# A matmul of 272 and one of 256 columns in place of two of 264, with x in rows of high and low

## Chip, cores and metric

One core of one Trainium2 chip. The metric is device time in microseconds (us) of one launch; the time before is 2108.19 us, the median of 3 runs (2107.79 to 2108.54).

## The reference

One step of a one-layer decoder for 264 tokens (256 of a prompt and 8 single ones), width 2048, all in fp32. A mixer (input projection to 7168, short gated convolution and retention, output projection) is followed by PEER, a retrieval of experts, and a last RMSNorm. What matters here is PEER's sum over experts:

```
u = u_tab[idx]
act = gelu(einsum('td,thkd->thk', xb, u))
w = gate * act
out = einsum('thk,thkd->td', w, v_tab[idx])
```

The table has 16384 experts, each with a row u and a row v of 2048. The kernel doesn't gather: it computes `x U^T` for all experts, takes the gelu, multiplies by a gate that is zero where a token didn't pick the expert, and multiplies the result by V.

## The kernel before

All activations lie transposed: 128 features or experts on the partitions, the 264 tokens (`T`) as columns. Every large product is made in three matmuls of type fp32r. An operand is split into a high part (the value rounded to fp32r) and a low part (the rest), and `half` adds `high x high`, `low weight x high` and `high weight x low` in PSUM. A weight tile is 128 output features by 2048 inputs, loaded in two halves of 8 rows of 128 x 128 (512 KB each, 688 halves in all). The path of a half: SP's queue loads it into `raw`, a ring of 4 (L523, L539); ScalarE casts it to `whi` (L640); VectorE subtracts and writes `wlo` (L1192); TensorE goes through the 8 rows with three matmuls each (L940, L941, L942). `lo_done` releases TensorE and the next load, `half_used` releases ScalarE's next cast. `whi` and `wlo` have a pitch of 136 words a row (`PITCH`), and all x operands are read from the last column to the first.

Stages, in order: heads' projections with retention beside them (moving operand `xghi`, `xglo`), the convolution's, the output projection (`xhi`, `xlo`), the queries (`xghi`, `xglo`), then PEER. In PEER a u tile (2 halves, 16 rows) gives 128 experts' scores in one bank; 7 groups of 8 u tiles lead, and 9 rounds (`MIXED`) follow, of 8 u tiles and 8 v tiles each; the last 7 groups have v tiles alone. A v group has 8 tiles of 2 halves with 8 rows, one row for each of the group's 8 expert tiles; each half fills one bank with one chunk j of the output, and VectorE adds the bank into `acc[:, j]` (`add_out`, L1827). So v's stages have 16 groups x 8 x 2 x 8 = 2048 rows. Their moving operand is the gated hidden value, in `wexp_hi` and `wexp_lo` in the mixed rounds and, in the last 7 groups, in halves of `xhi` and `xlo` (`expanded`; written at L884 and L1821 by ScalarE and VectorE in `weigh_hi` and `weigh`).

TensorE's other work is small: sums over partitions with plain fp32 (L972, L1020, L1024), turns and attention (L984 to L1013), query scores (L1068), and batches of 24 bf16 matmuls of 64 columns that build the gates (L1113).

Order on the engines is written out by hand: in each tile step, `ahead(r, k)` comes first and converts the two halves after next, then come gelu, gates and adds of the tile before. Banks 0 to 3 take turns for outputs; `bank_free` releases them.

x arrives in `acc` by four loads (`x_block`, L520); at the end `acc` is scaled and stored in six (L1883, L561).

Of the kernel before, what the change touches and what calls it, by code (L numbers as in the profile page):

```python
# [20 lines left out]
F32 = mybir.dt.float32  # L21
# [24 lines left out]

PITCH = P + T % P

SQ_RING = 4
# [161 lines left out]
def build(nc, halves, xT, conv_state, ret_state, norm_mix, conv_w, gn_g, gn_b, norm_ffn, keysT, norm_fin,  # L211
          consts, out_yT, out_conv, out_pret, out_sret):
    with ExitStack() as ctx:
        def sb(name, shape, dt=F32, scope=ctx):
            return scope.enter_context(nc.sbuf_tensor(name, shape, dt))
# [8 lines left out]

        xhi = sb("xhi", [P, CH, T], F32R)
        xlo = sb("xlo", [P, CH, T], F32R)
        acc = sb("acc", [P, CH, T])
        keep = sb("keep", [P, KEEP])
# [19 lines left out]

        xghi = sb("xghi", [P, CH, T], F32R, mix)
        xglo = sb("xglo", [P, CH, T], F32R, mix)  # L250
        tables = sb("tables", [P, NCONST - KEEP], F32, mix)
# [46 lines left out]
        scope.close()  # L298
        wexp_hi = sb("wexp_hi", [P, GROUP, T], F32R)
        wexp_lo = sb("wexp_lo", [P, GROUP, T], F32R)  # L300

# [197 lines left out]
        def wait_gates(eng, half):  # L499
            for i in range(2):  # L500
                eng.wait_ge(gates_stored[i], 16 * stored_of((half + 1) * BLOCKS, i))

        def expanded(buf):

            if buf is None:
                return wexp_hi, wexp_lo
            return xhi[:, buf * GROUP:(buf + 1) * GROUP], xlo[:, buf * GROUP:(buf + 1) * GROUP]

# [418 lines left out]
        def _(pe):  # L927
            def from_last(x):
                return x[..., ::-1] if len(x.shape) == 2 else x.rearrange("p a t -> p (a t)")[:, ::-1]

            def half(r, off, out, mh, ml, start, stop, waits=()):

                s = off % RING
                pe.wait_ge(lo_done, RING * r + off + 1)
                back = out[:, ::-1]
# [14 lines left out]

            def tile(r, k, o4, off, hi_, lo_, waits=({}, {}), between=None):

                out_free(o4, off)
                b = bank[off % BANKS][:, 0:T]
                half(r, 2 * k, b, [hi_[:, c, :] for c in range(HALF)], [lo_[:, c, :] for c in range(HALF)],
                     True, False, waits[0])
                if between:
                    between()
                half(r, 2 * k + 1, b, [hi_[:, HALF + c, :] for c in range(HALF)],
                     [lo_[:, HALF + c, :] for c in range(HALF)], False, True, waits[1])  # L960

# [64 lines left out]
            def head(h):  # L1026
                r, first = h * 2, isinstance(h, int) and h == 0
                tiles, att, _ = steps_of(h)
                for k, part in enumerate((turn, states, outputs, mean)):
                    if att:  # L1030
                        part(h - 1)
                    if tiles:
                        tile(r, k, h, k, xghi, xglo, norm_waits(0) if first and k == 0 else ({}, {}),
                             (lambda: sum_over_partitions(1)) if first and k == 2 else None)
                    elif loads_tiles(h):
                        tile(W_CONV // 2, k, W_CONV // BANKS, k, xghi, xglo)
                if att:
                    variance(h - 1)
# [7 lines left out]
            for k in range(BANKS, T_CONV):  # L1046
                tile(W_CONV // 2, k, W_CONV // BANKS, k, xghi, xglo)

            def out_tiles(i):
                first = isinstance(i, int) and i == 0  # L1050
                for k in range(4):
                    w = ({}, {})
                    if first and k == 0:
                        w = tuple({c: [(y_ready, y_turn(s * HALF + c) + 1)] for c in range(HALF)} for s in range(2))
                    if not first:
                        pe.wait_ge(x1_ready, i * 4 + k - 3)
                    tile(W_OUT // 2 + i * 2, k, FREED_U0 if first else None, k, xhi, xlo, w)

# [13 lines left out]
            def query_tiles(i):  # L1072
                first = isinstance(i, int) and i == 0
                for k in range(4):
# [3 lines left out]
                    else:  # L1078
                        pe.wait_ge(q_ready, i * 4 + k - 3)
                    b = bank[k][:, 0:T]  # L1080
                    r = W_Q // 2 + i * 2
                    half(r, 2 * k, b, [xghi[:, c, :] for c in range(HALF)], [xglo[:, c, :] for c in range(HALF)],
                         True, False, w[0])
                    if first and k == 0:
                        sum_over_partitions(2)
                    else:
                        if first and k == 1:
# [7 lines left out]
                        score(i * 4 + k - 1, (k - 1) % 2)  # L1095
                    half(r, 2 * k + 1, b, [xghi[:, HALF + c, :] for c in range(HALF)],
                         [xglo[:, HALF + c, :] for c in range(HALF)], False, True, w[1])

# [18 lines left out]
            for k in range(GROUP):  # L1117
                if k < BANKS:
                    pe.wait_ge(q_ready, SETS - BANKS + k + 1)
                    b = bank[k][:, 0:T]  # L1120
                    for s in range(2):
                        w = {c: [(norm_ready, CH + s * HALF + c + 1)] for c in range(HALF)} if k == 0 else {}
                        half(C_LEAD // 2, 2 * k + s, b, [xhi[:, s * HALF + c, :] for c in range(HALF)],
                             [xlo[:, s * HALF + c, :] for c in range(HALF)], s == 0, s == 1, w)
                else:
                    tile(C_LEAD // 2, k, FREED_U0, k, xhi, xlo)

            def lead_tile(g, k):
                tile(C_LEAD // 2 + g * (GROUP // 2), k, FREED_U0 + g * (GROUP // BANKS), k, xhi, xlo)

# [16 lines left out]
            def v_tiles(r, k0, o4, off0, g, buf, hook):  # L1147

                w_hi, w_lo = expanded(buf)
                for k in range(GROUP):  # L1150
                    for s in range(2):
                        off = off0 + 2 * k + s
                        out_free(o4, off)
                        w = {0: [(w_ready, (g + 1) * GROUP)]} if k == 0 and s == 0 else {}
                        half(r, 2 * (k0 + k) + s, bank[off % BANKS][:, 0:T], [w_hi[:, c] for c in range(GROUP)],
                             [w_lo[:, c] for c in range(GROUP)], True, True, w)
                    hook(k0 + k)

            def rounds(g):
# [7 lines left out]
                for k in range(GROUP):  # L1167
                    tile(r, k, o4, k, xhi, xlo)
                    hook(k)
# [786 lines left out]
```

## Time and profile before

| | |
|---|---|
| median of 3 runs | 2108.19 us |
| the profiled execution | 2108.31 us |
| its span, first to last instruction | 2106.5 us |
| granted TensorE clock, mean of the span | 0.998 |
| TensorE busy | 2085.1 us, 99% |
| VectorE, ScalarE, GpSimd busy | 1440.8, 961.2, 68.6 us |
| DMA engines | 418.39 MB, mean 199 GB/s |

Busy times of matmuls overlap, since they are pipelined: the page gives one matmul 283 ns where the next starts 120 ns behind it. How fast TensorE goes is read from starts in the timeline, or from a window's length over its count of matmuls. A row's PEclk is the granted clock, 1.00 at full speed (2.4 GHz).

### The profile page before, as it was taken

How to read it: one execution, taken by the hardware profiler on the slowest of the kernel's cores; microseconds unless marked ns; L12 is line 12 of the kernel's file. 1: busy time of each engine (PE TensorE's matmuls, PEld its weight loads, DVE VectorE, ACT ScalarE, POOL GpSimd, SP SyncE). 2: the span in 40 equal slices, each digit the busy share in tenths (PEclk: the TensorE clock that was granted, in tenths of full speed). 3: DMA queues.
4: the chain of work that ended last, by engine and by line, in shares of the span. 5: the costliest groups of instructions: out<-in, count | busy, mean ns of one | idle time of the engine just before them, and what ended most of it. 6: DMA issues, size and time to landing. Idle time of an engine off the chain costs nothing.

```text
span 2106.5 us, 46484 instructions
## 1 busy us (share of the span) xinstructions
PE 2085.1 (99%) x18585; PEld 2079.0 (99%) x18585; DVE 1440.8 (68%) x2701; ACT 961.2 (46%) x1343; POOL 68.6 (3%) x94
## 2 busy tenths in 40 slices
PE   8999999999999999999999999999999999999997
PEld 8999999999999999999999999999999999999997
DVE  8788876569988577754666666665645556666665
ACT  6666533445534344443434344444434344444444
POOL 1111000000000000000000000000000000000000
PEclk9999999999999999999999999999999999999999
DMA  8666555654455556675656565555655565655553
GB/s 297 222 217 217 194 180 182 201 180 156 166 190 180 180 187 215 214 243 182 201 192 216 194 207 199 201 205 195 207 196 200 180 213 207 213 202 205 206 178 125
DMA packets 115175, 418.39 MB, mean 199 GB/s; under 512 B 13600, under 2 KB 14112, under 8 KB 114752
## 3 DMA queue, kind: packets, MB, share of 16 engines
q1 hardware_dynamic: 100800, 365.29, 51.2%
q0 software_dynamic: 9888, 34.47, 5.0%
q10 hardware_dynamic: 4320, 16.22, 2.0%
q8 instruction: 128, 2.10, 0.4%
q14 instruction: 39, 0.32, 0.0%
HBM read 391.55 MB, written 24.29 MB: 197 GB/s over the span
## 4 chain that ended last, share of the span: by engine, by line
PE 97%; DVE 1%; DMA 0%; ACT 0%; issue 0%; DVEq 0%; SPq 0%; ACTq 0%
PE bank L940 31%; PE bank L942 31%; PE bank L941 31%; PE bank L1113 2%; DVE wlo L1192 1%; PE bank L1068 1%; DMA acc<-xT 0%; PE bank L1013 0%; ACT whi L640 0%; DMA raw<-halves 0%; DVE acc L1883 0%; PE bank L1024 0%; PE bank L1020 0%; ACT xghi L690 0%; PE bank L988 0%
## 5 line engine op out<-in xcount | busy, mean ns | idle before, releaser
L1192 DVE TENSOR_TENSOR wlo<-raw,whi 128x1024 fp32r<-128x1024 f32 x688 | 830.5, 1223 | 494.0 <-ACT whi L640 490.3
L640 ACT CAST whi<-raw 128x1024 fp32r<-128x1024 f32 x688 | 708.2, 1045 | 624.5 <-PE bank L942 619.1
L940 PE MATMUL bank<-xhi,whi 128*128 128x264 f32 x3200 | 912.4, 285 | 0.0
L942 PE MATMUL bank<-xlo,whi 128*128 128x264 f32 x3200 | 905.6, 283 | 0.0
L941 PE MATMUL bank<-xhi,wlo 128*128 128x264 f32 x3200 | 905.6, 283 | 0.0
L940 PEld LDWEIGHTS bank<-xhi,whi 128*128 128x128 f32 x3200 | 601.7, 188 | 0.0
L942 PEld LDWEIGHTS bank<-xlo,whi 128*128 128x128 f32 x3200 | 601.6, 188 | 0.0
L941 PEld LDWEIGHTS bank<-xhi,wlo 128*128 128x128 f32 x3200 | 600.8, 188 | 0.0
L940 PE MATMUL bank<-xghi,whi 128*128 128x264 f32 x1152 | 334.3, 290 | 9.1 <-DVE wlo L1192 9.1
L940 PE MATMUL bank<-wexp_hi,whi 128*128 128x264 f32 x1152 | 328.4, 285 | 0.0
L942 PE MATMUL bank<-xglo,whi 128*128 128x264 f32 x1152 | 327.3, 284 | 0.0
L941 PE MATMUL bank<-xghi,wlo 128*128 128x264 f32 x1152 | 327.2, 284 | 0.0
L942 PE MATMUL bank<-wexp_lo,whi 128*128 128x264 f32 x1152 | 326.0, 283 | 0.0
L941 PE MATMUL bank<-wexp_hi,wlo 128*128 128x264 f32 x1152 | 326.0, 283 | 0.0
L940 PEld LDWEIGHTS bank<-xghi,whi 128*128 128x128 f32 x1152 | 217.4, 189 | 9.6 <-DVE wlo L1192 9.1
L941 PEld LDWEIGHTS bank<-xghi,wlo 128*128 128x128 f32 x1152 | 217.7, 189 | 0.4
L942 PEld LDWEIGHTS bank<-xglo,whi 128*128 128x128 f32 x1152 | 217.2, 189 | 0.0
L941 PEld LDWEIGHTS bank<-wexp_hi,wlo 128*128 128x128 f32 x1152 | 216.6, 188 | 0.0
L940 PEld LDWEIGHTS bank<-wexp_hi,whi 128*128 128x128 f32 x1152 | 216.3, 188 | 0.0
L942 PEld LDWEIGHTS bank<-wexp_lo,whi 128*128 128x128 f32 x1152 | 216.2, 188 | 0.0
L845 ACT ACTIVATE hid<-bank 128x264 f32<-128x264 f32 x128 | 49.8, 389 | 203.2 <-PE bank L942 201.8
L1827 DVE TENSOR_TENSOR acc<-bank,acc 128x264 f32<-128x264 f32 x256 | 99.4, 426 | 49.0 <-PE bank L942 49.0
(217 smaller groups left out, 1124.9 us busy)
## 6 DMA issues: line engine op xcount, KB each, us to landing
raw<-halves SPq DMA_DIRECT2D x688, 512.0 KB, 3.6
hid<-gates ACTq DMA_DIRECT2D x30, 528.0 KB, 4.7
gates<-stage POOLq DMA_DIRECT2D x17, 768.0 KB, 7.3
s_old<-ret_state POOLq DMA_DIRECT2D x8, 512.0 KB, 7.1
vs_all<-values POOLq DMA_DIRECT2D x8, 512.0 KB, 5.6
ret_sample<-s_new POOLq DMA_DIRECT2D x8, 512.0 KB, 4.2
gates<-route_mem POOLq DMA_DIRECT2D x5, 768.0 KB, 7.4
acc<-xT SPq DMA_DIRECT2D x4, 528.0 KB, 6.8
```

Of the source, the lines that this page charges most:

```text
L640: nc.scalar.copy(whi[:, s], raw[:, s]).then_inc(hi_done, 1)
L845: nc.scalar.activation(hid[:, slot_of(g, k)], bank[b][:, 0:T].unsqueeze(1), ACT.Gelu)\
L940: nc.tensor.matmul(back, whi[:, s, c], high, start=start and c == 0, stop=False)
L941: nc.tensor.matmul(back, wlo[:, s, c], high, start=False, stop=False)
L942: mm = nc.tensor.matmul(back, whi[:, s, c], low, start=False, stop=stop and c == HALF - 1)
L1068: mm = nc.tensor.matmul(bank[4 + b][:, t * NK:(t + 1) * NK], qs[b][:, t * P:(t + 1) * P], keys_sb[:, j, :], start=True, stop=True)
L1113: mm = nc.tensor.matmul(o, onehot2[:, e, t], gated1[:, e, part, t], start=part == 0, stop=part == PARTS - 1)
L1192: v.tensor_tensor(wlo[:, s], raw[:, s], whi[:, s].bitcast(F32), ALU.subtract).then_inc(lo_done, 1)
L1827: v.tensor_tensor(acc[:, j, :], bank[off % BANKS][:, 0:T], acc[:, j, :], ALU.add)\
```

## The change

x's high and low part of one chunk come to lie in one row of 528 words (`xs`, `xg`, `wexp`), high first. `acc` becomes a view of `sums_mem`, whose rows have 8 more words (`SPILL` = 264 modulo 32). In v's stages, all groups but the last, `half` gets `spill`: the first matmul takes the 264 high columns and the first 8 low ones in one go (272) and writes 272 columns of the bank, so that the 8 low products have sums of their own behind the others; the third takes the other 256 low columns and adds them to bank columns 8 to 264. `add_out` adds 272 columns into `sums_mem`, and before the last group VectorE adds the 8 spilled ones to the first 8, for all chunks at once. In the last group and in all other stages the three matmuls have 264 columns as before. Row c of a half is put at `place_of(c)` of `whi` and `wlo` (0, 2, 4, 6, 1, 3, 5, 7) by the two conversions.

```diff
+def place_of(c):
+    return 2 * c % HALF + 2 * c // HALF
+
+SPILL = T % 32
...
-        xhi = sb("xhi", [P, CH, T], F32R)
-        xlo = sb("xlo", [P, CH, T], F32R)
-        acc = sb("acc", [P, CH, T])
+        xs = sb("xs", [P, CH, 2 * T], F32R)
+        xhi, xlo = xs[:, :, 0:T], xs[:, :, T:2 * T]
+        sums_mem = sb("sums_mem", [P, CH, T + SPILL])
+        acc = sums_mem[:, :, 0:T]
...
+        def placed(w, s):
+            return w[:, s].rearrange("p (b a) m -> p a b m", a=2)
+
+        def in_order(s):
+            return raw[:, s].rearrange("p (a b) m -> p a b m", a=2)
...
-                nc.scalar.copy(whi[:, s], raw[:, s]).then_inc(hi_done, 1)
+                nc.scalar.copy(placed(whi, s), in_order(s)).then_inc(hi_done, 1)
...
-            def half(r, off, out, mh, ml, start, stop, waits=()):
+            def half(r, off, bank_, x, c0, start, stop, waits=(), spill=False):
...
+                n = T + SPILL if spill else T
...
-                    high, low = from_last(mh[c]), from_last(ml[c])
-                    nc.tensor.matmul(back, whi[:, s, c], high, start=start and c == 0, stop=False)
-                    nc.tensor.matmul(back, wlo[:, s, c], high, start=False, stop=False)
-                    mm = nc.tensor.matmul(back, whi[:, s, c], low, start=False, stop=stop and c == HALF - 1)
+                    row, at = x[:, c0 + c, :], place_of(c)
+                    nc.tensor.matmul(bank_[:, 0:n][:, ::-1], whi[:, s, at], row[:, 0:n][:, ::-1],
+                                     start=start and c == 0, stop=False)
+                    nc.tensor.matmul(bank_[:, 0:T][:, ::-1], wlo[:, s, at], row[:, 0:T][:, ::-1], start=False, stop=False)
+                    mm = nc.tensor.matmul(bank_[:, n - T:T][:, ::-1], whi[:, s, at], row[:, n:2 * T][:, ::-1],
+                                          start=False, stop=stop and c == HALF - 1)
...
+                        half(r, 2 * (k0 + k) + s, bank[off % BANKS], rows_of(buf), 0, True, True, w, g < GROUPS - 1)
...
+            v.memset(sums_mem[:, :, T:T + SPILL], 0.0)
...
-                v.tensor_tensor(wlo[:, s], raw[:, s], whi[:, s].bitcast(F32), ALU.subtract).then_inc(lo_done, 1)
+                v.tensor_tensor(placed(wlo, s), in_order(s), placed(whi, s).bitcast(F32), ALU.subtract).then_inc(lo_done, 1)
...
-            def add_out(r, k, off, j):
+            def add_out(r, k, off, j, n=T + SPILL):
                 dve.wait_ge(half_used, RING * r + 2 * k + j % 2 + 1)
-                v.tensor_tensor(acc[:, j, :], bank[off % BANKS][:, 0:T], acc[:, j, :], ALU.add)\
+                v.tensor_tensor(sums_mem[:, j, 0:n], bank[off % BANKS][:, 0:n], sums_mem[:, j, 0:n], ALU.add)\
                     .then_inc(bank_free[off % BANKS], 1)
...
+            for b in range(BANKS):
+                dve.wait_ge(bank_free[b], FREED_TAIL + (GROUPS - 1 - MIXED) * (CH // BANKS))
+            ch.did(v.tensor_tensor(acc[:, :, 0:SPILL], acc[:, :, 0:SPILL], sums_mem[:, :, T:T + SPILL], ALU.add))
+            ch.wait()
             for k in range(GROUP):
...
-                    add_out(r, k, j, j)
+                    add_out(r, k, j, j, T)
```

## Rows read from the trace of the kernel before

**Rows 1.** The page's head and its chain that ended last (parts 1 and 4).
```profile
PE 2085.1 (99%) x18585; PEld 2079.0 (99%) x18585; DVE 1440.8 (68%) x2701; ACT 961.2 (46%) x1343; POOL 68.6 (3%) x94
...
PE 97%; DVE 1%; DMA 0%; ACT 0%; issue 0%; DVEq 0%; SPq 0%; ACTq 0%
PE bank L940 31%; PE bank L942 31%; PE bank L941 31%; PE bank L1113 2%; DVE wlo L1192 1%; PE bank L1068 1%; DMA acc<-xT 0%; PE bank L1013 0%; ACT whi L640 0%; DMA raw<-halves 0%; DVE acc L1883 0%; PE bank L1024 0%; PE bank L1020 0%; ACT xgh
```

**Rows 2.** The page's costliest groups (part 5): busy us, mean ns | idle before.
```profile
L1192 DVE TENSOR_TENSOR wlo<-raw,whi 128x1024 fp32r<-128x1024 f32 x688 | 830.5, 1223 | 494.0 <-ACT whi L640 490.3
L640 ACT CAST whi<-raw 128x1024 fp32r<-128x1024 f32 x688 | 708.2, 1045 | 624.5 <-PE bank L942 619.1
L940 PE MATMUL bank<-xhi,whi 128*128 128x264 f32 x3200 | 912.4, 285 | 0.0
...
L940 PE MATMUL bank<-xghi,whi 128*128 128x264 f32 x1152 | 334.3, 290 | 9.1 <-DVE wlo L1192 9.1
L940 PE MATMUL bank<-wexp_hi,whi 128*128 128x264 f32 x1152 | 328.4, 285 | 0.0
...
L1827 DVE TENSOR_TENSOR acc<-bank,acc 128x264 f32<-128x264 f32 x256 | 99.4, 426 | 49.0 <-PE bank L942 49.0
```

**Rows 3.** Windows: length, then busy us (count) of PE, PEld, DVE, ACT, POOL; PEclk, DMA share, GB/s.
```profile
25.00:260.00 235.00, 234.34 (x2075) 232.57 (x2074) 202.37 (x349) 145.73 (x216) 26.68 (x39) 1.00 0.66 218
1632.16:1678.34 46.18, 46.18 (x386) 46.18 (x385) 23.50 (x30) 17.04 (x17) 0.00 (x0) 1.00 0.54 183
1678.34:1724.53 46.19, 46.19 (x387) 46.19 (x385) 26.68 (x34) 21.56 (x31) 0.00 (x0) 1.00 0.61 206
1816.90:2047.80 230.90, 230.90 (x1922) 230.90 (x1921) 152.40 (x240) 99.15 (x122) 0.00 (x0) 1.00 0.58 202
```

**Rows 4.** Groups by line, v stage 1632.16 to 1678.34 us (L941, L942 alike).
```profile
L940 PE MATMUL bank<-wexp_hi,whi 128*128 128x264 f32 x128 | 36.4, 284 | 0.0
```

**Rows 5.** Timeline of TensorE in the tail: start us, length us, line.
```profile
2046.03 0.28 PE L940 MATMUL bank<-xhi,whi 128*128 128x264 f32 x1
2046.15 0.28 PE L941 MATMUL bank<-xhi,wlo 128*128 128x264 f32 x1
```

**Rows 6.** Timeline of TensorE's first matmuls, and the window over them (last row).
```profile
9.71 0.42 PE L942 MATMUL bank<-xglo,whi 128*128 128x264 f32 x1
9.93 0.42 PE L940 MATMUL bank<-xghi,whi 128*128 128x264 f32 x1
...
9.10:13.45 4.35, 4.35 (x20) 4.35 (x21) 3.91 (x9) 4.35 (x10) 0.76 (x2) 1.00 1.03 415
```

**Rows 7.** Timeline of TensorE around the fp32 sum of L1020 (264 columns).
```profile
56.20 0.61 PE L1020 MATMUL bank<-oT,keep 128*128 128x264 f32 x2
...
56.76 0.28 PE L941 MATMUL bank<-xghi,wlo 128*128 128x264 f32 x1
```

**Rows 8.** Timeline of TensorE around fp32 matmuls with 128 columns.
```profile
35.36 0.38 PE L984 MATMUL bank<-keep,vT 128*128 128x128 f32 x2
35.57 0.38 PE L986 MATMUL bank<-keep,kT 128*128 128x128 f32 x2
...
36.37 0.28 PE L941 MATMUL bank<-xghi,wlo 128*128 128x264 f32 x1
```

**Rows 9.** Timeline of TensorE's weight loads behind a batch.
```profile
1503.43 0.19 PEld L940 LDWEIGHTS bank<-xhi,whi 128*128 128x128 f32 x1
1503.54 0.19 PEld L941 LDWEIGHTS bank<-xhi,wlo 128*128 128x128 f32 x1
```

**Rows 10.** The page's DMA issues (part 6): count, KB each, us to landing.
```profile
raw<-halves SPq DMA_DIRECT2D x688, 512.0 KB, 3.6
...
s_old<-ret_state POOLq DMA_DIRECT2D x8, 512.0 KB, 7.1
```

**Rows 11.** Chain of waits at the start: start us, length us, what.
```profile
2.13 6.39 DMA acc<-xT
```

More of the change, by code:

```diff
@@ L247, in build @@
         mix = ExitStack()
-        xghi = sb("xghi", [P, CH, T], F32R, mix)
-        xglo = sb("xglo", [P, CH, T], F32R, mix)
+        xg = sb("xg", [P, CH, 2 * T], F32R, mix)
+        xghi, xglo = xg[:, :, 0:T], xg[:, :, T:2 * T]
         tables = sb("tables", [P, NCONST - KEEP], F32, mix)
@@ L298, in build @@
         scope.close()
-        wexp_hi = sb("wexp_hi", [P, GROUP, T], F32R)
-        wexp_lo = sb("wexp_lo", [P, GROUP, T], F32R)
+        wexp = sb("wexp", [P, GROUP, 2 * T], F32R)
         onehot1 = pair[:].rearrange("p a t -> p (a t)").bitcast(BF16)[:, 0:GB * SPAN].rearrange("p (t k) -> p t k", t=GB)
@@ L501, in wait_gates, with rows_of @@
                 eng.wait_ge(gates_stored[i], 16 * stored_of((half + 1) * BLOCKS, i))
+        def rows_of(buf):
+            return wexp if buf is None else xs[:, buf * GROUP:(buf + 1) * GROUP]
         def expanded(buf):
-            if buf is None:
-                return wexp_hi, wexp_lo
-            return xhi[:, buf * GROUP:(buf + 1) * GROUP], xlo[:, buf * GROUP:(buf + 1) * GROUP]
+            rows = rows_of(buf)
+            return rows[:, :, 0:T], rows[:, :, T:2 * T]
+        def placed(w, s):
+            return w[:, s].rearrange("p (b a) m -> p a b m", a=2)
+        def in_order(s):
+            return raw[:, s].rearrange("p (a b) m -> p a b m", a=2)
         def u_tile(g):
@@ L927, in _ @@
         def _(pe):
-            def from_last(x):
-                return x[..., ::-1] if len(x.shape) == 2 else x.rearrange("p a t -> p (a t)")[:, ::-1]
-            def half(r, off, out, mh, ml, start, stop, waits=()):
+            def half(r, off, bank_, x, c0, start, stop, waits=(), spill=False):
                 s = off % RING
                 pe.wait_ge(lo_done, RING * r + off + 1)
-                back = out[:, ::-1]
+                n = T + SPILL if spill else T
                 for c in range(HALF):
@@ L949, in out_free, with tile @@
                 pe.wait_ge(bank_free[off % BANKS], o4 + off // BANKS)
-            def tile(r, k, o4, off, hi_, lo_, waits=({}, {}), between=None):
+            def tile(r, k, o4, off, x, waits=({}, {}), between=None):
                 out_free(o4, off)
-                b = bank[off % BANKS][:, 0:T]
-                half(r, 2 * k, b, [hi_[:, c, :] for c in range(HALF)], [lo_[:, c, :] for c in range(HALF)],
-                     True, False, waits[0])
+                b = bank[off % BANKS]
+                half(r, 2 * k, b, x, 0, True, False, waits[0])
                 if between:
                     between()
-                half(r, 2 * k + 1, b, [hi_[:, HALF + c, :] for c in range(HALF)],
-                     [lo_[:, HALF + c, :] for c in range(HALF)], False, True, waits[1])
+                half(r, 2 * k + 1, b, x, HALF, False, True, waits[1])
             def sum_over_partitions(n):
@@ L1032, in head @@
                     if tiles:
-                        tile(r, k, h, k, xghi, xglo, norm_waits(0) if first and k == 0 else ({}, {}),
+                        tile(r, k, h, k, xg, norm_waits(0) if first and k == 0 else ({}, {}),
                              (lambda: sum_over_partitions(1)) if first and k == 2 else None)
                     elif loads_tiles(h):
-                        tile(W_CONV // 2, k, W_CONV // BANKS, k, xghi, xglo)
+                        tile(W_CONV // 2, k, W_CONV // BANKS, k, xg)
                 if att:
@@ L1046, in _ @@
             for k in range(BANKS, T_CONV):
-                tile(W_CONV // 2, k, W_CONV // BANKS, k, xghi, xglo)
+                tile(W_CONV // 2, k, W_CONV // BANKS, k, xg)
             def out_tiles(i):
@@ L1056, in out_tiles @@
                         pe.wait_ge(x1_ready, i * 4 + k - 3)
-                    tile(W_OUT // 2 + i * 2, k, FREED_U0 if first else None, k, xhi, xlo, w)
+                    tile(W_OUT // 2 + i * 2, k, FREED_U0 if first else None, k, xs, w)
             out_tiles(0)
@@ L1079, in query_tiles @@
                         pe.wait_ge(q_ready, i * 4 + k - 3)
-                    b = bank[k][:, 0:T]
+                    b = bank[k]
                     r = W_Q // 2 + i * 2
-                    half(r, 2 * k, b, [xghi[:, c, :] for c in range(HALF)], [xglo[:, c, :] for c in range(HALF)],
-                         True, False, w[0])
+                    half(r, 2 * k, b, xg, 0, True, False, w[0])
                     if first and k == 0:
@@ L1095, in query_tiles @@
                         score(i * 4 + k - 1, (k - 1) % 2)
-                    half(r, 2 * k + 1, b, [xghi[:, HALF + c, :] for c in range(HALF)],
-                         [xglo[:, HALF + c, :] for c in range(HALF)], False, True, w[1])
+                    half(r, 2 * k + 1, b, xg, HALF, False, True, w[1])
             query_tiles(0)
@@ L1119, in _ @@
                     pe.wait_ge(q_ready, SETS - BANKS + k + 1)
-                    b = bank[k][:, 0:T]
                     for s in range(2):
                         w = {c: [(norm_ready, CH + s * HALF + c + 1)] for c in range(HALF)} if k == 0 else {}
-                        half(C_LEAD // 2, 2 * k + s, b, [xhi[:, s * HALF + c, :] for c in range(HALF)],
-                             [xlo[:, s * HALF + c, :] for c in range(HALF)], s == 0, s == 1, w)
+                        half(C_LEAD // 2, 2 * k + s, bank[k], xs, s * HALF, s == 0, s == 1, w)
                 else:
-                    tile(C_LEAD // 2, k, FREED_U0, k, xhi, xlo)
+                    tile(C_LEAD // 2, k, FREED_U0, k, xs)
             def lead_tile(g, k):
-                tile(C_LEAD // 2 + g * (GROUP // 2), k, FREED_U0 + g * (GROUP // BANKS), k, xhi, xlo)
+                tile(C_LEAD // 2 + g * (GROUP // 2), k, FREED_U0 + g * (GROUP // BANKS), k, xs)
             with pe.Fori(1, TURN_AT // GROUP) as g:
@@ L1147, in v_tiles @@
             def v_tiles(r, k0, o4, off0, g, buf, hook):
-                w_hi, w_lo = expanded(buf)
                 for k in range(GROUP):
@@ L1154, in v_tiles @@
                         w = {0: [(w_ready, (g + 1) * GROUP)]} if k == 0 and s == 0 else {}
-                        half(r, 2 * (k0 + k) + s, bank[off % BANKS][:, 0:T], [w_hi[:, c] for c in range(GROUP)],
-                             [w_lo[:, c] for c in range(GROUP)], True, True, w)
+                        half(r, 2 * (k0 + k) + s, bank[off % BANKS], rows_of(buf), 0, True, True, w, g < GROUPS - 1)
                     hook(k0 + k)
@@ L1167, in rounds @@
                 for k in range(GROUP):
-                    tile(r, k, o4, k, xhi, xlo)
+                    tile(r, k, o4, k, xs)
                     hook(k)
```

## Prediction

> **What bounds the kernel now.** I read the head of the page first: TensorE is busy for 99% of the span and 97% of the chain that ended last is its own work, nearly all of it the three lines of `half` [rows 1]. So time is made by the number of matmuls and by how far apart they start. The costliest groups [rows 2] give the counts: 16512 matmuls of 264 columns come from the three lines (3 x (3200 + 1152 + 1152)), all of one shape, and their own waits are small: 9.1 us once. The "mean ns of one" there (283 to 290) is a modelled length of pipelined work and must not be used as a price; the price is the distance between starts. That I take from windows over stages without other TensorE work (the rows are a part of the heads' stage, a v stage, a u stage and five groups of the tail): a v stage of 46.18 us holds 128 of each line, 384 matmuls, hence 0.1203 us each, and 230.9 us of the tail hold 1922, hence 0.1201 [rows 3, 4]. The timeline of the tail shows the same steps of 0.12 one by one [rows 5], and repeats them throughout. In both windows VectorE (23.5 of 46.2, 152.4 of 230.9 us) and ScalarE (17.0, 99.2) have room, and the DMA engines are at 0.54 to 0.58 [rows 3]: nothing but TensorE's own pace counts there. Every v row costs three such steps, 0.361 us.
>
> **What a step of 0.120 us is made of** decides this case, since the change keeps the columns of a row's three matmuls at 792 (264 + 264 + 264 before, 272 + 264 + 256 after). Four rows bear on it.
> (a) In the first microseconds the same matmuls start 0.22 us apart [rows 6]; 264 columns at the lower level, 1.2 GHz, take 0.220 us. So there the step is the columns alone, with nothing on top. (The clock column of that window reads 1.00, but the steps say the lower level.) At 2.4 GHz the columns would take 0.110, and the step is 0.120: something adds 0.010 that doesn't show at the lower level.
> (b) Plain fp32 matmuls of 264 columns: L1020 has two instructions of two passes each, and from the first to L941, two starts on, is 0.56 us, less one ordinary step of 0.12 leaves 0.44, so 0.11 a pass [rows 7]. The extra 0.010 isn't there, so it belongs to the fp32r form.
> (c) Eight fp32 matmuls with 128 columns (two passes each): 36.37 - 35.36 = 1.01, less 0.12, is 0.89, or 0.111 each, 0.1075 for the first two [rows 8]. Each brings its own 128 x 128 four-byte weights, so such a load needs at most that. After a batch, L940's load and L941's start 0.11 apart while no columns stream [rows 9]. So the weights' load is a floor of about 0.11, but not the 0.120.
> (d) 0.120 us is 288 columns at 2.4 GHz, and 288 is 264 rounded up to whole groups of 32 (9 groups).
> Rounding in some feed that only limits the fp32r form at the upper clock fits (a) to (d) all, to the nanosecond; a constant or proportional extra fits them too, but then the round figure is chance.
>
> **The change, part by part.**
> 1. Spill matmuls. v rows that get the new split: 15 groups of 8 tiles, 2 halves and 8 rows, 1920 (the 16th group keeps 264 and 264, 128 rows). By groups of 32, L940's 272 columns take 9 groups as 264 do: 0. L942's 256 columns take 8: 0.1067, which is under the load's floor. Bounds for its step: 0.1067 to 0.120 (no gain at all; the proportional reading is below). I take 0.110, by the loads of [rows 8, 9], whose values lie at 0.1075 to 0.111. That is 0.010 x 1920 = 19.2 us off; with 0.1067 it would be 25.6, with 0.111 17.3.
> 2. `place_of` and x in rows of 528. All 16512 matmuls read the same number of columns and weights; only the distances in memory between weight row and x row change. By the buffers' sizes in the code, `xlo` lies 4224 words behind `xhi` (0 modulo 128) and `wexp_lo` 2112 behind `wexp_hi` (64 modulo 128), `xghi` elsewhere again; the stages that read each of them step alike [rows 3, 7]. I take 0; upper bound 0.8 ns on each (see the rivals), lower bound nothing, as no step shows a saving from place.
> 3. ScalarE's and VectorE's conversions (688 of 1.045 and 1.223 us [rows 2]) now run over two strides in place of one. Same elements; I take 0. If each grew by 10% it would be 0.12 us on VectorE; in the heads' stage, where VectorE is fullest (202.4 of 235 us [rows 3]), 80 of them are 9.6 us and its spare 32.6. In the start, before 40 us, the chain runs through a handful of them, at most 1 us.
> 4. `add_out` takes 272 columns, 426 ns x 8/264 = 13 ns x 240 = 3.1 us on VectorE, hidden in its idle time; were the cover gone, 3 us. The one addition of the spilled sums is put between groups 14 and 15: two converted halves (5.8 us of TensorE work) are ready there, so it costs 0. Queued behind it are VectorE's next conversions, and TensorE would wait for those, but only if it took over about 4 us; it handles 16 x 8 elements a partition.
> 5. `acc` gets a row pitch of 272: the four loads of x and the output's first four stores no longer run over 4224 contiguous bytes a partition but over 1056. The start's chain runs through such a load (6.39 us [rows 11]). With 4 KB runs a 512 KB load lands in 3.6 us, with runs of 512 bytes (`s_old`) in 7.1 [rows 10]; so the price lies between 0 and 3.5 us for the start, and 1056 bytes lie nearer to the short end in length but four loads share the queue. I take 1.0, and 0.5 for the first stores at the end (the last two store one chunk each, as before): +1.5, bounds 0 and +4.5.
> 6. The clearing of the spill columns is one short VectorE instruction before x arrives: 0. SP's queue keeps its four loads of x and six stores, and no DMA is added on any queue.
>
> Sum against the profiled execution's 2108.31 us: 2108.3 - 19.2 + 1.5 = 2090.6. The median of the runs is 0.12 lower, so 2090.5. A faster TensorE uses converted halves every 2.81 us in place of 2.89; VectorE's 152.4 of 230.9 us in the tail becomes 152.4 + 1.0 of about 224.5, still room.
>
> The Trainium skill ("TensorE: Matmul & The Clock Gate", Back-to-back issue gap) gives a warm step as N / 2.4 plus about 2.5 ns: 112.5 ns for 264 columns, where the trace has 120.1 to 120.3, so it is short by 7.7 here. By it 272 would add as much as 256 saves, and the sum would be 2109.7 in place of 2090.5. Its weight load ("LDWEIGHTS", P / 1.2, 107 ns) would put the floor of part 1 at 107.
>
> **Rivals.**
> A, **the step is proportional or constant on top** (0.110 + 0.010 for 264): 272 costs what 256 gives back. Then nothing is gained and the +1.5 stays: 2109.7. For it: (a) shows that columns aren't rounded in TensorE's own count, and (b) that fp32 isn't rounded. Against it: no reason why fp32r should add just 0.010 when fp32 adds nothing. A step set wholly by loads of 0.120 gives the same time; against that stand the 0.11 of rows 8 and 9. This is also the case in which the change doesn't do what its columns promise, and the Trainium skill's rule above leads here.
> B, **groups counted by address.** If the groups are 128 bytes of memory and not of the instruction, a 256-column low part touches 8 only where it starts on a boundary. Rows are 528 words apart, 528 = 16 modulo 32, so every other row starts in the middle and takes 9: half the gain, 9.6 us: 2108.3 - 9.6 + 1.5 - 0.1 = 2100.1. The trace of before can't speak: all 264-column rows touch 9 either way.
> C, **slower: the new distances disturb the reads.** Weight row 4 used to lie one pitch behind row 3; now row c and its x row agree only for c below 4, and everywhere the low part lies 264 words off. L941 and L942 start 0.120 apart from the next, and the mean is 0.1203, so L940's step is 0.1208 [rows 4]: 0.8 ns is the one difference that the reads show today. If it came upon the other 11008 matmuls too and part 1 gave nothing, that is 8.8 + 1.5: 2118.5. It decides from 0.3 ns a matmul on (no gain), or 1.2 ns (with the gain). Against it: the different distances of part 2, which step alike.
>
> **How the numbers follow.** Forecast 0.54, A 0.18, B 0.11, C 0.17. The forecast's own range is 2083 (25.6 off, start free) to 2095 (17.3 off, +4.5). The range has to take in A and B and leaves out C: 2083 to 2110.5. A measurement of this kernel can tell about 0.2%, 4.2 us, from no change. Faster by more: forecast and B, 0.65; within: A, 0.18; slower: C, 0.17.
>
> **What would show it.** The v stage's window of 384 matmuls, now 46.18 us: 44.9 by the forecast, 45.5 by B, with steps of 0.12, 0.12, 0.11 in the timeline (B: alternating), 46.2 by A. The u stages' 46.19 should not move (C: 46.5 or more). TensorE's first matmul at 9.10 should come by 1 us later or less. VectorE's and ScalarE's conversions should keep 1.22 and 1.05 us. I am wrong if the third matmul's step stays at 0.120 or the first's grows to 0.123; if both move, the groups aren't 32.

## The result, and the profile after

The changed kernel takes 2119.44 us (median of 5 runs, 2119.10 to 2120.65) against 2108.19 before: ratio 1.0054, 95% interval 1.0040 to 1.0069. It is slower by 11.25 us, where 2090.5 was forecast. The profiled execution took 2120.65 us, with a span of 2118.6, 12.1 over that of before.

The page of the changed kernel, its head, its chain and the groups that answer to [rows 1, 2]:

```profile
span 2118.6 us, 46492 instructions
...
PE 2095.0 (99%) x18585; PEld 2089.0 (99%) x18585; DVE 1443.3 (68%) x2703; ACT 961.5 (45%) x1343; POOL 68.5 (3%) x94
...
PE 97%; DVE 1%; DMA 1%; ACT 0%; SPq 0%; issue 0%; DVEq 0%; ACTq 0%
...
L1201 DVE TENSOR_TENSOR wlo<-raw,whi 128x1024 fp32r<-128x1024 f32 x688 | 830.5, 1223 | 499.8 <-ACT whi L656 496.1
L656 ACT CAST whi<-raw 128x1024 fp32r<-128x1024 f32 x688 | 708.8, 1046 | 633.9 <-PE bank L957 626.7
...
L954 PE MATMUL bank<-wexp,whi 128*128 128x272 f32 x1152 | 335.2, 291 | 0.0
L956 PE MATMUL bank<-wexp,wlo 128*128 128x264 f32 x1152 | 328.8, 285 | 0.0
...
L957 PE MATMUL bank<-wexp,whi 128*128 128x256 f32 x1152 | 322.6, 280 | 0.0
...
L1836 DVE TENSOR_TENSOR sums_mem<-bank,sums_mem 128x272 f32<-128x272 f32 (+1 forms) x256 | 101.3, 433 | 49.1 <-PE bank L957 49.1
```

The same 18585 matmuls, conversions of 1223 and 1046 ns where they were 1223 and 1045, and the chain is TensorE's own work as before. So no slower conversion took the time, and outside the start and the end no new wait did. The windows that answer to [rows 3] (v stage, u stage, five groups of the tail):

```profile
1639.99:1686.70 46.71, 46.71 (x386) 46.71 (x385) 23.63 (x30) 17.09 (x17) 0.00 (x0) 1.00 0.53 181
1686.70:1733.00 46.30, 46.30 (x386) 46.30 (x385) 26.68 (x34) 21.56 (x31) 0.00 (x0) 1.00 0.59 206
1826.23:2058.76 232.53, 232.53 (x1922) 232.53 (x1921) 153.01 (x240) 99.08 (x122) 0.00 (x0) 1.00 0.58 200
```

The v stage went from 46.18 to 46.71 us where 44.9 was forecast, the u stage from 46.19 to 46.30 where nothing should move, the tail's five groups from 230.90 to 232.53. Now the steps of the v stage one by one, rows c = 1 and c = 5 of a half, from the timeline of TensorE (start us, length us):

```profile
1640.35 0.29 PE L954 MATMUL bank<-wexp,whi 128*128 128x272 f32 x1
1640.48 0.29 PE L956 MATMUL bank<-wexp,wlo 128*128 128x264 f32 x1
1640.61 0.28 PE L957 MATMUL bank<-wexp,whi 128*128 128x256 f32 x1
1640.72 0.29 PE L954 MATMUL bank<-wexp,whi 128*128 128x272 f32 x1
...
1641.82 0.29 PE L954 MATMUL bank<-wexp,whi 128*128 128x272 f32 x1
1641.94 0.28 PE L956 MATMUL bank<-wexp,wlo 128*128 128x264 f32 x1
1642.06 0.28 PE L957 MATMUL bank<-wexp,whi 128*128 128x256 f32 x1
1642.18 0.29 PE L954 MATMUL bank<-wexp,whi 128*128 128x272 f32 x1
```

In the first row the steps are 0.13, 0.13 and 0.11 (272, 264, 256 columns; 0.37 together); in the second 0.12, 0.12 and 0.12 (0.36). The timeline rounds to 0.01, so from here on a step in ns is the mean distance from a matmul's start to the next one's over all rows of that kind in the trace, batches left out. For 272, 264 and 256 columns it is 125.8, 123.3 and 115.9 in the mixed rounds, 365.0 ns a row, and 123.5, 121.9 and 117.9 in the tail, 363.3. Before it was 120.8, 120.0 and 120.0 everywhere, 360.8. In the stages that still use 264 columns it is 120.8, 120.0 and 120.9: the third step, of the low part, got 0.85 ns longer.

By place, the profiled execution's 12.1 us are: 1.62 before the 24th matmul starts, 1.84 from there to the first v stage, 7.58 from there to the start of the last matmul, 1.04 behind it. At the start of this execution x comes later and TensorE begins at 10.36 in place of 9.10:

```profile
6.38 1.73 ACT L706 ACTIVATE xg<-sums_mem,gains 128x264 fp32r<-128x264 f32 x4 [4.13 <-DMA sums_mem<-xT]
...
10.36 0.59 PE L954 MATMUL bank<-xg,whi 128*128 128x264 f32 x1 [10.36 <-DVE wlo L1201]
```

### The profile page after: what moved, and what is told of

It is laid out like the page before. It is cut to its first block, busy times and chain, and to the rows that moved or that the text cites. A ratio compares the mean times of both kernels' runs of the same rounds, so it can differ in the third digit from the quotient of the medians.

```text
span 2118.6 us, 46492 instructions
## 1 busy us (share of the span) xinstructions
PE 2095.0 (99%) x18585; PEld 2089.0 (99%) x18585; DVE 1443.3 (68%) x2703; ACT 961.5 (45%) x1343; POOL 68.5 (3%) x94
## 4 chain that ended last, share of the span: by engine, by line
PE 97%; DVE 1%; DMA 1%; ACT 0%; SPq 0%; issue 0%; DVEq 0%; ACTq 0%
PE bank L954 32%; PE bank L956 31%; PE bank L957 31%; PE bank L1125 2%; DMA raw<-halves 1%; PE bank L1082 1%; DVE wlo L1201 0%; PE bank L1027 0%; ACT whi L656 0%; DVE sums_mem L1896 0%; PE bank L1038 0%; PE bank L1034 0%; PE bank L1002 0%; PE bank L1012 0%; SPq L539 0%
## 5 line engine op out<-in xcount | busy, mean ns | idle before, releaser
L1201 DVE TENSOR_TENSOR wlo<-raw,whi 128x1024 fp32r<-128x1024 f32 x688 | 830.5, 1223 | 499.8 <-ACT whi L656 496.1
L656 ACT CAST whi<-raw 128x1024 fp32r<-128x1024 f32 x688 | 708.8, 1046 | 633.9 <-PE bank L957 626.7
L954 PE MATMUL bank<-xs,whi 128*128 128x264 f32 (+1 forms) x3200 | 915.2, 286 | 0.0
L956 PE MATMUL bank<-xs,wlo 128*128 128x264 f32 x3200 | 907.0, 283 | 0.0
L957 PE MATMUL bank<-xs,whi 128*128 128x264 f32 (+1 forms) x3200 | 907.0, 283 | 0.0
L957 PEld LDWEIGHTS bank<-xs,whi 128*128 128x128 f32 x3200 | 601.4, 188 | 0.0
L956 PEld LDWEIGHTS bank<-xs,wlo 128*128 128x128 f32 x3200 | 601.3, 188 | 0.0
L954 PEld LDWEIGHTS bank<-xs,whi 128*128 128x128 f32 x3200 | 601.3, 188 | 0.0
L954 PE MATMUL bank<-xg,whi 128*128 128x264 f32 x1152 | 334.2, 290 | 10.4 <-DVE wlo L1201 10.4
L954 PE MATMUL bank<-wexp,whi 128*128 128x272 f32 x1152 | 335.2, 291 | 0.0
L956 PE MATMUL bank<-wexp,wlo 128*128 128x264 f32 x1152 | 328.8, 285 | 0.0
L957 PE MATMUL bank<-xg,whi 128*128 128x264 f32 x1152 | 328.4, 285 | 0.0
L956 PE MATMUL bank<-xg,wlo 128*128 128x264 f32 x1152 | 327.2, 284 | 0.0
L954 PEld LDWEIGHTS bank<-xg,whi 128*128 128x128 f32 x1152 | 217.8, 189 | 10.7 <-DVE wlo L1201 10.4
L957 PEld LDWEIGHTS bank<-wexp,whi 128*128 128x128 f32 x1152 | 219.3, 190 | 0.0
L957 PEld LDWEIGHTS bank<-xg,whi 128*128 128x128 f32 x1152 | 217.6, 189 | 0.0
L954 PEld LDWEIGHTS bank<-wexp,whi 128*128 128x128 f32 x1152 | 216.5, 188 | 0.0
```

The source lines that it names most:

```text
L656: nc.scalar.copy(placed(whi, s), in_order(s)).then_inc(hi_done, 1)
L954: nc.tensor.matmul(bank_[:, 0:n][:, ::-1], whi[:, s, at], row[:, 0:n][:, ::-1], start=start and c == 0, stop=False)
L956: nc.tensor.matmul(bank_[:, 0:T][:, ::-1], wlo[:, s, at], row[:, 0:T][:, ::-1], start=False, stop=False)
L957: mm = nc.tensor.matmul(bank_[:, n - T:T][:, ::-1], whi[:, s, at], row[:, n:2 * T][:, ::-1], start=False, stop=stop and c == HALF - 1)
L1201: v.tensor_tensor(placed(wlo, s), in_order(s), placed(whi, s).bitcast(F32), ALU.subtract).then_inc(lo_done, 1)
```

## The experiments

Each time is compared with runs of the kernel before on the same chip, 2108.42 us (first four experiments), 2108.45 (next four) and 2108.45 (last two). Experiments 1, 6, 7 and 9 are one execution each, made for its trace.

**1. How a step depends on its columns.** The kernel before; in the u stages of the nine mixed rounds `wide` takes `COLUMNS[g]` columns in each matmul:

```diff
-                    tile(r, k, o4, k, xhi, xlo)
+                    out_free(o4, k)
+                    wide(r, 2 * k, k, 0, True, False)
+                    wide(r, 2 * k + 1, k, HALF, False, True)
```

> The kernel before, but the 128 rows of each u stage in the nine mixed rounds run with 264, 256, 272, 280, 288, 304, 320, 352 and 384 columns in all three matmuls (columns over 264 read on into the next row and land in unused bank columns; the round with 256 leaves out the 8 single tokens' scores). Theory A (a step is the columns at 2.4 GHz plus 0.010 us): steps 0.120, 0.117, 0.123, 0.127, 0.130, 0.137, 0.143, 0.157, 0.170. Rival, groups of 32 columns: 0.120, 0.110, 0.120, 0.120, 0.120, 0.133, 0.133, 0.147, 0.160. Rival, bound by a weight load of 0.120: flat at 0.120 up to 288 columns.

The u stages' windows with 264, 352 and 384 columns:

```profile
913.36:959.55 46.19, 46.19 (x387) 46.19 (x385) 26.16 (x33) 22.70 (x33) 0.00 (x0) 1.00 0.68 229
1612.35:1673.25 60.90, 60.90 (x386) 60.90 (x385) 26.68 (x34) 21.83 (x31) 0.00 (x0) 1.00 0.46 156
1719.44:1785.68 66.24, 66.24 (x387) 66.24 (x385) 26.68 (x34) 22.01 (x31) 0.00 (x0) 1.00 0.44 145
```

and seven starts of 384 columns in a row, from the timeline:

```profile
1730.00 0.34 PE L1178 MATMUL bank<-xhi,wlo 128*128 128x384 f32 x1
...
1731.06 0.34 PE L1178 MATMUL bank<-xhi,wlo 128*128 128x384 f32 x1
```

1.06 us over six steps is 0.177. Over rows c = 1 to 6 the means for 256, 264, 272, 280, 288, 304, 320, 352 and 384 columns are 118.1, 120.3, 124.8, 130.3, 133.5, 140.3, 146.9, 161.0 and 175.8 ns. Groups of 32 columns are refuted (272 costs 4.5 ns more than 264, 288 costs 13), and so is a load of 0.120 (flat up to 288). But the constant 0.010 of rival A falls too: 384 stands at 0.176 and not at 0.170. Rival B falls with the groups: at a pitch of 264 words the rows start at four different offsets within 32 words, and rows of 272 columns take 374 to 375 ns at all of them.

**2. The layout without the spill.** The changed kernel with equal counts:

```diff
-                        half(r, off, bank, rows, 0, True, True, w, g < GROUPS - 1)
+                        half(r, off, bank, rows, 0, True, True, w, False)
-            def add_out(r, k, off, j, n=T + SPILL):
+            def add_out(r, k, off, j, n=T):
```

> The changed kernel with 264, 264 and 264 columns in v's stages too; x in rows of 528, the new places of the weights and acc's pitch stay. If the loss is from the new distances in memory, v rows keep their excess (0.365 us in the mixed rounds) and the time stays near 2119. If the excess in v comes only with unequal column counts, v rows return to 0.361 to 0.362 us and what is left is start, end and the low part's 0.8 ns: 2108.2 + 2.7 + 3 to 4, so about 2114 to 2115.

2114.89 us, ratio 1.0030 (1.0018 to 1.0042). The same three windows:

```profile
1635.95:1682.24 46.29, 46.29 (x386) 46.29 (x385) 23.50 (x30) 17.09 (x17) 0.00 (x0) 1.00 0.55 183
1682.24:1728.54 46.30, 46.30 (x387) 46.30 (x385) 26.68 (x34) 21.60 (x31) 0.00 (x0) 1.00 0.62 206
1821.12:2052.59 231.47, 231.47 (x1922) 231.47 (x1921) 152.38 (x240) 99.33 (x122) 0.00 (x0) 1.00 0.61 201
```

The v stage falls back from 46.71 to 46.29 but not to 46.18; all stages are now alike, 0.11 us longer per 128 rows, with steps of 120.8, 120.0 and 120.9. Over 5504 rows 0.85 ns is 4.7 us. So the further excess of v rows comes with unequal counts, and the layout costs the 0.85 ns in every stage.

**3. Plain places.** The changed kernel with row c of a half at place c:

```diff
 def place_of(c):
-    return 2 * c % HALF + 2 * c // HALF
+    return c
```

> The changed kernel with row c of the weights at place c as before. If the places matter (weight row and x row no longer advance alike), the steps of all stages change: slower than 2119 if the new places had helped, as little as 2116 if they had hurt. If nothing depends on places, 2119 again and the same steps row by row.

2121.99 us, 1.0064 (1.0047 to 1.0080). v stage and u stage:

```profile
1640.80:1687.41 46.61, 46.61 (x386) 46.61 (x385) 23.62 (x30) 17.04 (x17) 0.00 (x0) 1.00 0.58 181
1687.41:1733.82 46.41, 46.41 (x386) 46.41 (x385) 26.70 (x34) 21.57 (x31) 0.00 (x0) 1.00 0.63 205
```

The u stage is 0.11 longer than with `place_of`, the v stage 0.10 shorter. With equal counts, rows now differ from one another: 360.0 to 365.9 ns where they had all been 361.7. So the places had helped where columns are equal, and the pairing of weight row and x row does matter: nothing but the places of the weights has changed.

**4. acc's pitch alone.**

```diff
-        acc = sb("acc", [P, CH, T])
+        sums_mem = sb("sums_mem", [P, CH, T + T % 32])
+        acc = sums_mem[:, :, 0:T]
```

> The kernel before with acc in rows of 272, nothing else. The first matmul of the changed kernel starts at 10.36 us in place of 9.10 and its end takes 1.05 us longer. If that is the short runs of the loads and stores, this kernel shows both: 2108.2 + 1.65 + 1.05 = 2110.9. If the conversions' strides did it, 2108.2.

2109.99 us, 1.0006 (0.9997 to 1.0016). The interval takes in no change, but all ten runs (2109.69 to 2110.58) lie above all sixteen of the kernel before (at most 2109.48), so I count the 1.6 us between the medians. The end is as expected, the start only in part. SP's six stores of the output take 5.77 us to issue, where the kernel before needs 4.91, and the last two 3.4 us to land, where they took 2.8. The end of the timeline, and the two last stores among the DMA issues:

```profile
2098.40 4.90 DVE L1884 TENSOR_TENSOR sums_mem<-sums_mem,stats 128x1056 f32<-128x1056 f32 x6
2099.69 5.77 SPq L562 DMA_DIRECT2D yT<-sums_mem  x6
```

```profile
yT<-sums_mem SPq DMA_DIRECT2D x2, 132.0 KB, 3.4
```

Behind the last matmul this kernel is 1.04 us longer, just as the changed one is. That leaves about 0.5 us of the 1.6 for the start. One trace can't show so little there: in the seven traces with acc as it was (the kernel before and experiments 1, 5, 7, 8, 9 and 10) the 24th matmul starts between 13.96 and 14.88 us, here at 14.74, in experiments 2 and 3, which have all the layout, at 14.33 and 13.81. So the changed kernel's 15.58, 1.62 later than before, is for the most part its one execution, which is also 1.2 us over the median of its runs.

**5. Only 256 columns in the third matmul of v**, in the old layout, the low products of the first 8 tokens left out:

```diff
-                    mm = nc.tensor.matmul(back, whi[:, s, c], low, start=False, stop=stop and c == HALF - 1)
+                    mm = nc.tensor.matmul(out[:, skip:T][:, ::-1], whi[:, s, c], low[:, 0:T - skip], start=False, stop=stop and c == HALF - 1)
```

> The kernel before in its own layout; in the 1920 v rows the third matmul takes the last 256 columns of the low part (the low part's products of the first 8 tokens are left out), the first two keep 264. If a column costs 0.45 ns wherever it is taken away, a v row goes from 0.361 to 0.357 us and the time to 2108.4 - 7 = 2101. If unequal counts bring excesses of their own, as in the changed kernel, the row stays at 0.361 or goes over it and the time is 2108 to 2116. Groups of 32 would give 2108.4 - 19 = 2089.

2104.16 us, 0.9980 (0.9971 to 0.9990). v stage and tail:

```profile
1628.66:1674.42 45.76, 45.76 (x387) 45.76 (x385) 23.50 (x30) 17.04 (x17) 0.00 (x0) 1.00 0.56 185
1812.55:2043.48 230.93, 230.93 (x1922) 230.93 (x1921) 152.38 (x240) 99.12 (x122) 0.00 (x0) 1.00 0.59 202
```

Two answers in one run. In the mixed rounds a row falls to 357.5 ns (121.3, 120.0, 116.3), 3.3 less. In the tail it stays at 360.8: the third step is 115.8, but the second grew to 125.0. Four starts there, with steps of 0.12, 0.13 and 0.11:

```profile
2039.87 0.28 PE L940 MATMUL bank<-xhi,whi 128*128 128x264 f32 x1
2039.99 0.29 PE L941 MATMUL bank<-xhi,wlo 128*128 128x264 f32 x1
2040.12 0.28 PE L942 MATMUL bank<-xlo,whi 128*128 128x256 f32 x1
2040.23 0.28 PE L940 MATMUL bank<-xhi,whi 128*128 128x264 f32 x1
```

For TensorE's v matmuls the two stages differ only in where x lies. So taking 8 columns away gives 3.3 ns (1152 rows, 3.8 of the 4.3 us), and an excess that depends on place can take all of it back.

**6. Is it the distance?** In the changed kernel wexp's rows begin 4 words further on with each mixed round:

```diff
+            if buf is None:
+                return wexp_mem[:, 4 * g:4 * g + GROUP * 2 * T].rearrange("p (a t) -> p a t", a=GROUP)
```

> The changed kernel, but in mixed round g (0 to 8) the rows of wexp begin 4 x g words further on. If the excess of v rows (0.3678 us against 0.3616 for two halves of the rows) comes from the distance between x row and weight row, the pattern over the 8 rows moves with g and v stages of different rounds differ in length (46.3 to 47.2 us). If it comes from the counts alone, all nine keep 46.7 us.

v stages shifted by 0, 4 and 8 words (the second and third with batches in them, 2.4 us each):

```profile
961.38:1008.09 46.71, 46.71 (x386) 46.71 (x385) 23.63 (x30) 17.09 (x17) 0.00 (x0) 1.00 0.55 181
1056.79:1106.12 49.33, 49.33 (x458) 49.18 (x457) 29.27 (x45) 18.50 (x20) 1.18 (x1) 1.00 0.56 189
1154.82:1203.73 48.91, 48.91 (x459) 48.77 (x457) 29.36 (x45) 18.50 (x20) 1.15 (x1) 1.00 0.57 190
```

The second and third differ by 0.42 us with the same work, and over all nine, batches taken off, the lengths run from 46.5 to 46.95, a narrower spread than expected. The pattern over the 8 rows of a half moves: with 0 words 368, 368, 369, 368, 362, 361, 362, 362 ns; with 8 words 362, 362, 362, 362, 371, 359, 371, 360. The latter is the tail's pattern in the changed kernel (362, 362, 362, 362, 371, 359, 371, 359), and by the buffers' sizes in the code 8 words is what brings wexp to the tail's distance from the weights modulo 64 words (56 before the shift; xs has 0). Here x rows move and weight rows stay; in experiments 3 and 8 it is the other way round, and the pattern moves as well. So how the excess lies over the rows goes with the distance between x row and weight row.

**7. Which reading is in the way.** The kernel before, u stages of different kinds:

```diff
+                    m = kind if isinstance(kind, int) else P
+                    turn_ = 1 if kind == 'forward' else -1
+                    w2 = whi if kind == 'whi' else wlo
```

> The kernel before; the u stage of rounds 0 to 8 runs plain; with weights of 96, 64, 32 columns (the experts behind them are left out); with x read first column to last; with the high weights in place of the low ones; with the high x in place of the low one; plain; plain. If the 0.010 us over 264 columns at 2.4 GHz is a conflict between the reading of weights and of x, fewer weight columns bring the step from 0.120 towards 0.110. If it belongs to the fp32r stream itself, the step stays at 0.120 with all of them. Reading forward: 0.120 if the direction doesn't matter, more if the two readings meet.

u stages 0 to 5: plain, 96, 64, 32 weight columns, forward, high weights twice. All but the first have batches, which take 2.4 us of a stage.

```profile
913.42:959.61 46.19, 46.19 (x387) 46.19 (x386) 26.15 (x33) 22.69 (x33) 0.00 (x0) 1.00 0.65 223
1005.79:1055.13 49.34, 49.34 (x458) 49.11 (x457) 32.24 (x49) 23.11 (x34) 1.18 (x1) 1.00 0.59 200
1103.72:1152.17 48.45, 48.45 (x458) 48.14 (x457) 32.23 (x49) 23.02 (x34) 1.15 (x1) 1.00 0.64 214
1200.76:1249.11 48.35, 48.35 (x459) 43.33 (x457) 32.23 (x49) 23.01 (x34) 1.15 (x1) 1.00 0.64 213
1297.69:1346.73 49.04, 49.04 (x458) 48.90 (x457) 32.23 (x49) 23.13 (x34) 1.15 (x1) 1.00 0.61 210
1395.32:1443.90 48.58, 48.58 (x458) 48.44 (x457) 32.23 (x49) 23.10 (x34) 1.15 (x1) 1.00 0.63 213
```

With 64 or 32 weight columns a row still takes 361 ns, and so it does with the high weights in place of the low ones and, in stage 6, with the high x in place of the low one. So the 10 ns over 264 columns at 2.4 GHz don't shrink with the weights that are loaded; that they belong to the fp32r stream is what is left, and is argued. But 96 weight columns give 367 to 368 ns and reading forward 363 to 366: an excess over 361 comes both from how the weights are read and from how x is read.

**8. A pitch of 128 words** for the weights:

```diff
-PITCH = P + T % P
+PITCH = P
```

> The kernel before with weight rows 128 words apart in place of 136, so that weight rows and x rows (264 words) no longer advance alike modulo 128. If the pairing of places sets the excess, rows differ from one another in all stages and the time goes up by 5 to 100 us; if places play no part with equal counts, 2108.4.

2117.58 us, 1.0042 (1.0026 to 1.0059). v and u stage:

```profile
1639.32:1685.72 46.40, 46.40 (x387) 46.40 (x385) 23.48 (x30) 17.06 (x17) 0.00 (x0) 1.00 0.52 182
1685.72:1732.12 46.40, 46.40 (x386) 46.40 (x385) 26.67 (x34) 21.55 (x31) 0.00 (x0) 1.00 0.60 205
```

Rows with equal counts run from 360.8 to 365.9 ns, so equal counts alone don't keep rows at 361: here weight rows advance by 128 words and x rows by 264, and modulo 128 that is no longer the same. This is the kernel before with one constant changed, 9.1 us slower.

**9. The slope without the weights' part.** As experiment 1, with 32 weight columns and counts up to 512:

```diff
-                        nc.tensor.matmul(back, whi[:, s, c], high, start=start and c == 0, stop=False)
+                        nc.tensor.matmul(back, whi[:, s, c, 0:32], high, start=start and c == 0, stop=False)
```

> As the column series, but each matmul has weights of 32 columns only (experts behind them are left out), so that the reading of weights is short, and the counts are 264, 256, 272, 288, 320, 352, 384, 448, 512. If a step is proportional to the columns at 0.4545 to 0.4585 ns each: 0.120, 0.117, 0.124, 0.132, 0.146, 0.161, 0.175, 0.204, 0.234. If it is the columns at 2.4 GHz plus a constant 0.010: 0.120, 0.117, 0.123, 0.130, 0.143, 0.157, 0.170, 0.197, 0.223.

Starts six steps apart with 288 columns, and then 512 columns:

```profile
1202.88 0.30 PE L1177 MATMUL bank<-xhi,whi 128*32 128x288 f32 x1
...
1203.66 0.30 PE L1177 MATMUL bank<-xhi,whi 128*32 128x288 f32 x1
```

```profile
1759.95 0.40 PE L1178 MATMUL bank<-xhi,wlo 128*32 128x512 f32 x1
...
1761.35 0.40 PE L1178 MATMUL bank<-xhi,wlo 128*32 128x512 f32 x1
```

The means for 264, 256, 272, 288, 320, 352, 384, 448 and 512 columns are 120.3, 118.1, 124.7, 131.4, 146.9, 160.3, 175.8, 204.7 and 233.6 ns. Over the columns at 2.4 GHz that is 10.3, 11.4, 11.4, 11.4, 13.6, 13.6, 15.8, 18.1 and 20.3: all but the first are multiples of 2.26 ns, 5 of them at 256 to 288 columns, 6 at 320 and 352, 7, 8 and 9 at 384, 448 and 512. That is one for each 64 columns and one more. It isn't the whole rule: with 128 weight columns (experiment 1) 280, 288 and 304 columns have 13.6, 13.5 and 13.6 over, six of them, where 288 has five here. A column costs 0.455 to 0.461 ns in this series and up to 0.465 in experiment 1, so moving 8 from one matmul to another gives nothing. Of the counts tried 264 has the least excess, and leaving it costs: by this series 272 + 264 + 256 makes 363.1 ns a row, against 360.8 for three times 264. Over the 1920 rows that is 4.4 us (an estimate), about what the uneven split costs in the changed kernel (4.5).

**10. The low part 8 words on**, in the old layout:

```diff
-        xlo = sb("xlo", [P, CH, T], F32R)
+        xlo = sb("xlo", [P, CH * T + 8], F32R)[:, 8:].rearrange("p (a t) -> p a t", a=CH)
```

> The kernel before with xlo 8 words further on (all that lies behind it moves by 8 as well), nothing else. In the layout of the change the low part lies 264 = 8 modulo 128 words behind the high part and its step is 0.8 ns longer. If that distance is the cause, the third step of the stages that read xhi and xlo goes from 120.0 to 120.9 ns and the time up by up to 2.8. If not, 2108.4.

2108.93 us, 1.0001 (0.9992 to 1.0011). v and u stage:

```profile
1632.94:1679.13 46.19, 46.19 (x387) 46.19 (x385) 23.49 (x30) 17.06 (x17) 0.00 (x0) 1.00 0.56 183
1679.13:1725.31 46.18, 46.18 (x386) 46.18 (x385) 26.67 (x34) 21.55 (x31) 0.00 (x0) 1.00 0.62 206
```

A miss. In the stages that read xlo the third step does become 120.9, as in the new layout, but the first falls from 120.8 to 120.0, and the row stays at 360.9. So which step is the longer one goes with the place of the low part, but in the new layout two steps are longer and here one. What decides between one and two is open.

## Why the prediction was wrong

The account, from medians: acc's pitch 1.6 us (experiment 4), rows of high and low with the new places 4.9 (experiment 2 less 4), the uneven split 4.5 (the changed kernel less experiment 2), together 11.0 against 2108.42. The prediction had 1.5, 0 and -19.2 for them.

**Part 1** failed, and with it reading (d). I took 272 columns at no cost and 256 at 0.110 us, 19.2 us off in all; measured, the split puts 4.5 us on. In the v stage the third step did fall, to 115.9 ns, but the first grew to 125.8 and the second to 123.3. In experiments 1 and 9, 272 cost 4.4 to 4.5 ns more than 264 and 256 gave 2.2 back. That is the prediction's own sign of being wrong: the first step grew over 0.123. "288 columns at 2.4 GHz" fitted 120.0 to the nanosecond and was chance: 264 columns with an excess of 10.3 ns. My own reading (a) spoke against groups, since 264 columns at the lower level take 0.22 (the level read off the steps, where the clock column has 1.00), and I explained it away with a feed that only limits at the upper level. The weights' load as a floor of 0.11 was never tested, because no step came nearer than 115.8 ns. Its two readings don't show one either: in [rows 8] two passes of 128 columns make 0.107 us at 2.4 GHz by themselves, so they bound the load from above only, and in [rows 9] L940's matmul starts at 1503.46, ahead of L941's load at 1503.54, so columns did stream. A number that matches one hypothesis exactly, with one shape in the trace, wasn't worth 0.54.

**Part 2** failed as well: I took 0 for the places. All steps of the trace of before were alike, at several distances, and I read that as "distance doesn't matter". Experiments 3, 6 and 8 show that it matters; the kernel before has its rows alike only while its pitch of 136 makes weight rows and x rows advance together (experiment 8). The layout of the change makes the third step 0.85 ns longer in every row, 4.7 us; what in it does so stays open, since moving the low part alone gave nothing (experiment 10). It keeps the common advance only for rows 0 to 3. With equal counts that costs nothing, rows 4 to 7 take 362 ns like the others (experiment 2); with v's uneven counts rows go from 359 to 371 ns by place, and the mean is 365.0 ns in the mixed rounds and 363.3 in the tail.

**Parts 3, 4 and 6** held: conversions 1223 and 1046 ns, `add_out` and the memset hidden, no new wait. The one addition of the spilled sums took 0.29 us at 2059.5 and held nothing up: between 2050 and 2095 us no two matmuls start over 0.14 us apart. **Part 5** was right in its sum and by luck: 1.5 taken, 1.6 measured, but of that 1.04 at the end, to which I had given 0.5, and about 0.5 at the start, to which I had given 1.0. Its upper bound of +4.5 isn't added up: its terms give 3.5 for the start and name none for the end.

**The rivals.** A was right that the split gains nothing, but it put the split's cost at 0 where it was 4.5 us and left out the layout's 4.9, so its 2109.7 is 9.7 us short. The Trainium skill's rule ("TensorE: Matmul & The Clock Gate", Back-to-back issue gap) led there, and the trace agrees on the missing gain, but not on the size: its 2.5 ns on top were 10.3 to 20.3 here, growing with the columns. C, with a chance of 0.17, named places in memory and so one of the two things that made it slower. That its 2118.5 lies near 2119.4 is in good part luck: 0.8 ns on two more steps of each row were 0.85 ns on one, which is half of its 8.8 us, and the other half came from the uneven counts, v rows paying 1.6 to 3.3 ns beyond that. The u stage's 46.30 us lies between the 46.19 of the forecast and the 46.5 that C asked for. B is refuted with the groups.

A version better than both kernels didn't come up: the kernels tried that do all the work have 792 columns a row, and no stage with all its work done had a mean row under the 360.8 ns of the kernel before.

## What to carry to other kernels

Before columns are moved between matmuls, measure how a step depends on their number: one kernel with a series of counts shows it, here to within the few ns a row that places add or take, and a trace with a single count can't tell rounding from a proportional or a constant part. Rows of weights and of x that are read at the same time have a distance; a trace in which all steps are alike may show a pairing that was set up, not one that doesn't matter. Change the layout alone first, with equal counts, and read its steps in a stage that the change should leave as it is.

## What of the hardware was unexpected

- An fp32r matmul at the upper clock level takes 0.455 to 0.465 ns a column from 256 to 512 columns, 9 to 12% over 2.4 GHz. With weights of 32 columns in place of 128 it was the same at 256, 264, 272, 320 and 384 columns, and 2.1 ns less only at 288 and 0.7 at 352 (experiments 1, 7, 9); plain fp32 took 0.11 us for a pass of 264 [rows 7].
- Weight columns can cost by being fewer: with 96 in place of 128, rows took 367 to 368 ns in place of 361, with 64 or 32 they took 361 (experiment 7).
- Reading x from first column to last cost 2 to 5 ns a row (experiment 7), a weight pitch of 128 words in place of 136 cost 9.1 us (experiment 8).
- With a row pitch of 272 words in place of 264, the first four of the six last stores run over 1056 bytes in place of up to 4224; SP's six issues took 0.86 us longer and the end 1.04 us. The last two, whose runs are as before, landed in 3.4 us in place of 2.8 (experiment 4).
